# A decoder layer on one core: the feed-forward's up products by quarters, seven block products for eight, on 18 of 22 column pairs

## What is computed

```
h   = RMSNorm(x)
u   = causal_dwconv(h @ w_up, ffn_conv)        # w_up: 1024 x 5632, width 3
gate, up = split(u)                            # 2816 columns each
x   = x + RMSNorm((silu(gate) * up) @ w_down)  # w_down: 2816 x 1024
```

## Time and profile before

| | us |
|---|---|
| median of 3 runs | 1547.7 |
| lowest and highest | 1547.31, 1548.53 |
| the profiled execution, its own time | 1546.41 |
| its span, first to last instruction | 1544.7 |
| PE busy | 1502.6 |
| DVE busy | 898.1 |
| ACT busy | 655.0 |
| POOL busy | 179.3 |

### The profile page before, as it was taken

How to read it: one execution, slowest core, us unless ns; L and a number is a source line. 1 busy time by engine, 2 the same in 40 slices (tenths; PEclk the granted TensorE clock), 3 DMA queues, 4 the chain that set the end, 5 groups by cost and what they waited for, 6 DMA issues and landing times.

```text
span 1544.7 us, 19459 instructions
## 1 busy us (share of the span) xinstructions
PE 1502.6 (97%) x7515; PEld 1265.8 (82%) x7515; DVE 898.1 (58%) x1371; ACT 655.0 (42%) x1151; POOL 179.3 (12%) x200
## 2 busy tenths in 40 slices
PE   5999999999989999999999999999999999999996
PEld 4777888788879998878888888888888888888885
DVE  6675536360158885466876664335967666334666
ACT  5433456321247785355443333224333333224344
POOL 3000011000067772000100000000200000000110
PEclk8999999999989999999999999999999999999998
DMA  7542425636223332633323332333232333223222
GB/s 217 81 94 35 43 88 148 159 99 111 83 78 108 111 104 90 217 89 89 109 85 93 96 102 94 101 112 97 85 107 83 100 100 98 97 97 114 91 96 96
DMA packets 169657, 158.16 MB, mean 102 GB/s; under 512 B 19608, under 2 KB 131422, under 8 KB 169566
## 3 DMA queue, kind: packets, MB, share of 16 engines
q1 hardware_dynamic: 169312, 156.82, 36.2%
q10 hardware_dynamic: 254, 0.10, 0.0%
HBM read 134.88 MB, written 22.02 MB: 102 GB/s over the span
## 4 chain that ended last, share of the span: by engine, by line
PE 93%; DVE 2%; ACT 2%; DMA 1%; issue 1%; POOL 0%; SPq 0%; ACTq 0%; DVEq 0%; POOLq 0%
PE psum L1915 10%; PE psum L1914 10%; PE psum L1913 10%; PE psum L1839 9%; PE psum L1841 9%; PE psum L1840 9%; PE psum L559 5%; PE psum L561 5%; PE psum L560 5%; PE psum L1198 4%; PE psum L1252 3%; PE psum L614 3%; PE psum L616 3%; PE psum L615 3%; DMA w_raw<-in_w_in 1%
## 5 line engine op out<-in xcount | busy, mean ns | idle before, releaser
L144 DVE TENSOR_TENSOR w_wlo<-w_raw,w_whi 128x1024 fp32r<-128x1024 f32 x202 | 261.2, 1293 | 541.9 <-ACT w_whi L138 541.8
L138 ACT ACTIVATE w_whi<-w_raw 128x1024 fp32r<-128x1024 f32 x202 | 213.9, 1059 | 634.9 <-PE psum L1915 282.2
L1913 PE MATMUL psum<-m_hi,w_whi 128*128 128x512 f32 x704 | 274.2, 390 | 0.0
L1915 PE MATMUL psum<-m_hi,w_wlo 128*128 128x512 f32 x704 | 273.9, 389 | 0.0
L1914 PE MATMUL psum<-m_lo,w_whi 128*128 128x512 f32 x704 | 273.9, 389 | 0.0
L1839 PE MATMUL psum<-w_whi,m_hi 128*128 128x512 f32 x592 | 231.2, 391 | 1.6 <-DVE w_wlo L144 0.9
L1840 PE MATMUL psum<-w_wlo,m_hi 128*128 128x512 f32 x592 | 230.4, 389 | 0.0
L1841 PE MATMUL psum<-w_whi,m_lo 128*128 128x512 f32 x592 | 230.4, 389 | 0.0
L1915 PEld LDWEIGHTS psum<-m_hi,w_wlo 128*128 128x128 f32 x704 | 132.1, 188 | 27.4
L1913 PEld LDWEIGHTS psum<-m_hi,w_whi 128*128 128x128 f32 x704 | 132.1, 188 | 27.4
L1914 PEld LDWEIGHTS psum<-m_lo,w_whi 128*128 128x128 f32 x704 | 132.1, 188 | 27.3
(11 more groups left out here) (303 smaller groups left out, 2126.0 us busy)
## 6 DMA issues: line engine op xcount, KB each, us to landing
w_raw<-in_w_up SPq DMA_DIRECT2D x88, 512.0 KB, 3.9
w_raw<-in_w_down SPq DMA_DIRECT2D x44, 512.0 KB, 3.7
w_raw<-in_w_in SPq DMA_DIRECT2D x36, 512.0 KB, 6.2
w_raw<-in_w_out SPq DMA_DIRECT2D x16, 512.0 KB, 4.5
w_raw<-in_w_ple_gate SPq DMA_DIRECT2D x16, 512.0 KB, 3.9
gate_rows<-rows_stage SPq DMA_DIRECT2D x24, 256.0 KB, 2.1
x_tiles<-in_x SPq DMA_DIRECT2D x8, 512.0 KB, 8.5
x<-in_x SPq DMA_DIRECT2D x8, 512.0 KB, 6.1
```

What stands on the lines that cost most here:

```text
L138: act.activation(self.whi[j % self.RING][:], self.raw[j % self.RAW][:], ACT.Copy).then_inc(self.rounded, 1)
L144: dve.tensor_tensor(self.wlo[j % self.RING][:], self.raw[j % self.RAW][:], self.whi[j % self.RING][:].bitcast(F32), ALU.subtract).then_inc ...
L1913: pe.matmul(out, wh[:, part], hi[:, kt, :], start=(kt == 0), stop=False)
L1915: ins = pe.matmul(out, wl[:, part], hi[:, kt, :], start=False, stop=(kt == KT - 1))
```

## The change

The up products of 18 of the 22 column pairs are no longer made for one token half after the other, but for both together. The operands are cut in two along the inner dimension, the tokens, and gate against up, which gives blocks of 2 by 2 by 2, and the eight block products become seven with the sums of Winograd's form. PE works in pieces: a piece is one weight block of 128x512 by one block of h (or a sum of blocks), 4 inner blocks by 3 matmuls. A pair has seven pieces, in the order B11, T1, T2, B21, T3, B22, T4; the T are sums. New work for a pair: POOL makes four sums of weight blocks (`Units.sum`) and two joins of results (`pool_join`); DVE makes seven remainders of 128x512, five joins that read PSUM, four taps and one gate over 1024 tokens (`dve_pairs`); ACT makes seven roundings of 128x512, three copies out of PSUM, the first tap of both lines and silu (`act_pairs`). The ring holds four pieces: `round(n)` waits until piece n-4 is multiplied.

The other four pairs are done as before, half after half, ahead of the 18 (`pe_plain`, 16 tiles in 32 pieces of 12 matmuls), and there POOL makes the remainders of the weights. In this stretch DVE and ACT make the sums of h. f1 is transposed after tiles 6 and 8 of 16, kt 0 to 3 and kt 4 to 7; f0 in two parts before the last two slabs of the output projection.

The gated values go to DRAM (`g_rows`), and are loaded again by 256 KB, each block once for each token half, into four buffers (`w_sums`) from which they are split (`load_g`, `act_split`). The residual goes to DRAM and comes back too. The down products of the first half run over row slabs as before; those of the second half run over two column halves of `w_down`, each in 11 slabs of two row blocks, and the splits of all 22 blocks fall in the first column half, two a slab. x0 is transposed in the second column half.

The core of the diff:

```diff
+
+    def ring(self, j):
+
+        return (j + (j >= self.flip)) % self.RING
 
...
+    RING, RAWS, PLAIN = 4, 4, 4
+    TILES = 4 * PLAIN
+    PAIRS = FT - PLAIN
+    STEPS = 7
+    B11, T1, T2, B21, T3, B22, T4 = range(STEPS)
+    N_PLAIN = 2 * TILES
...
+    def sum(self, pool, s, which):
...
+        b11, b21, b12, b22 = (self.block(s, u, half) for u in range(2) for half in range(2))
+        sums, n = self.sums[s % 2], 4 * s
+        if which == self.T1:
+            for u in range(2):
+                self.landed(pool, self.tile(s, u))
...
+            ins = pool.tensor_tensor(sums[:, 0, :], b12, b11, ALU.subtract)
+        elif which == self.T2:
+            pool.wait_ge(self.made, n + 1)
+            ins = pool.tensor_tensor(sums[:, 1, :], sums[:, 0, :], b22, ALU.subtract)
+        elif which == self.T3:
+            ins = pool.tensor_tensor(b12, b22, b12, ALU.subtract)
+        else:
+            pool.wait_ge(self.made, n + 2)
+            pool.wait_ge(self.rest, self.STEPS * s + self.T1 + 1)
+            ins = pool.tensor_tensor(sums[:, 0, :], b21, sums[:, 1, :], ALU.add)
+        ins.then_inc(self.made, 1)
...
+    def round(self, act, n):
...
+        if n < self.RING:
+            self.multiplied.wait(act, ("slab", self.at - 2 + n // 2))
+        else:
+            self.multiplied.wait(act, ("unit", n - self.RING))
+        act.activation(self.home(n)[0], self.source(n), ACT.Copy).then_inc(self.rounded, 1)
...
+    def remainder(self, eng, n):
...
+        hi, lo = self.home(n)
+        eng.wait_ge(self.rounded, n + 1)
+        eng.tensor_tensor(lo, self.source(n), hi.bitcast(F32),
+                          ALU.subtract).then_inc(self.plain_rest if n < self.N_PLAIN else self.rest, 1)
...
                     self.pe_natural(pe, f"outp{half}", first["outp", half] + n * KT // 2 + i, (2 * i, 2 * i + 1), (n,),
                                     of(self.hi[half]), of(self.lo[half]), 0, KT - 1)
-        for half in range(2):
-            self.pe_up(pe, half)
-            for kt in range(FT):
-                slot = kt % KT
-                pe.wait_ge(s["split_lo"], half * FT + kt + 1)
-                ghi, glo = self.hi[half], self.lo[half]
-                self.pe_natural(pe, f"down{half}", first["down", half] + kt, (kt,), (0, 1),
-                                lambda _, t: ghi[:, slot, t * P:(t + 1) * P], lambda _, t: glo[:, slot, t * P:(t + 1) * P],
+        self.pe_plain(pe, 0)
+        self.pe_plain(pe, 1)
+        self.pe_pairs(pe)
+        for kt in range(FT):
+            pe.wait_ge(s["split_lo"], kt + 1)
+            self.pe_natural(pe, "down0", first["down", 0] + kt, (kt,), (0, 1), *self.g_halves(0), 0, FT - 1)
+        for n in range(2):
+            for i in range(FT // 2):
+                if n == 0:
+                    pe.wait_ge(s["split_lo"], FT + 2 * i + 2)
+                self.pe_natural(pe, "down1", first["down", 1] + n * FT // 2 + i, (2 * i, 2 * i + 1), (n,), *self.g_halves(1),
                                 0, FT - 1)
+                if n * FT // 2 + i in self.X0_TURNS:
+                    for group in self.added:
+                        pe.wait_ge(group, self.add_count("down0", self.HT - 1))
...
+    def pe_piece(self, pe, n, out, hi, lo, start, stop, *keys, fresh=None):
+
+        self.units.ready(pe, n)
+        wh, wl = self.units.home(n)
+        for kt in range(KT // 2):
+            if fresh:
+                fresh(kt)
+            part = slice(kt * P, (kt + 1) * P)
+            pe.matmul(out, wh[:, part], hi(kt), start=(start and kt == 0), stop=False)
+            pe.matmul(out, wh[:, part], lo(kt), start=False, stop=False)
+            ins = pe.matmul(out, wl[:, part], hi(kt), start=False, stop=(stop and kt == KT // 2 - 1))
+        self.multiplied.mark(ins, ("unit", n), *keys)
...
+    def pe_pairs(self, pe):
+        s, units = self.s, self.units
+        h = lambda half, at: (lambda kt: self.hi[half][:, at + kt, :], lambda kt: self.lo[half][:, at + kt, :])
+        two = lambda ap, at: (lambda kt: ap[:, at, kt, :], lambda kt: ap[:, at + 1, kt, :])
+        moving = {Units.B11: h(1, 0), Units.T1: two(self.s1, 0), Units.T2: two(self.s23, 0), Units.B21: h(1, 4),
+                  Units.T3: two(self.s23, 2), Units.B22: h(0, 0), Units.T4: h(0, 4)}
+        first_use = {Units.T1: 4, Units.T2: 8, Units.T3: 12, Units.B22: 16}
+        for c in range(Units.PAIRS):
+            for q in range(Units.STEPS):
+                key = ("pair", c, q)
+                out = self.banks.open(pe, key, (Units.STEPS * c + q) % 8)
+                if c == 0 and q in first_use:
+                    pe.wait_ge(s["sum_lo"], first_use[q])
+                self.pe_piece(pe, units.number(c, q), out, *moving[q], True, True, key)
...
+        self.act_plain(act)
+        self.act_pairs(act)
+        j = first["down", 0]
+        for kt in range(FT - 1):
+            slabs.round(act, j + kt + 2, m)
+            self.act_split(act, kt + 2)
+        for t in range(self.HT):
+            self.act_out(act, "down0", t, 0)
+        self.act_split(act, FT + 1)
+        j = first["down", 1]
+        slabs.round(act, j + 1, m)
+        for i in range(FT - 1):
+            slabs.round(act, j + i + 2, m)
+            if i + 1 < FT // 2:
+                self.act_split(act, FT + 2 * i + 2)
+                self.act_split(act, FT + 2 * i + 3)
...
+    def act_pairs(self, act):
+        s, units, m = self.s, self.units, self.multiplied
+        base, late = 2 * Units.PLAIN, slice(self.PAD + HALF, self.PAD + SEQ)
+        for c in range(Units.PAIRS):
+            n = units.number(c, 0)
+            if c == 0:
+                self.act_plain_line(act, 1, base - 1)
+            else:
+                self.act_tap_up(act, c - 1)
+                self.act_gate_line(act, c - 1)
+            units.round(act, n + 3)
+            key = ("pair", c, Units.B11)
+            m.wait(act, key)
+            if c:
+                self.banks.released(act, ("pair", c - 1, Units.T2))
+                act.wait_ge(s["joined"], 2 * c - 1)
+            self.banks.release(act.activation(self.copies[0][:], self.banks.of(key), ACT.Copy), key)
+            units.round(act, n + 4)
+            if c:
+                self.act_tap_gate(act, c - 1)
+            units.round(act, n + 5)
+            if c == 0:
+                self.act_smooth(act, base - 1, self.acc[0], self.FREED + 2 * base - 1)
+            else:
+                self.act_smooth(act, base + c - 1, self.long_acc[0], self.FREED + 2 * (base + c))
+            units.round(act, n + 6)
+            key = ("pair", c, Units.B21)
+            m.wait(act, key)
+            act.wait_ge(s["freed"], self.FREED + 2 * (base + c))
+            self.banks.release(act.activation(self.long_line[0][:, late], self.banks.of(key), ACT.Copy), key)
+            units.round(act, n + 7)
+            units.round(act, n + 8)
+            if c == Units.PAIRS - 1:
+                m.wait(act, ("unit", n + Units.T3))
+                self.slabs.round(act, self.first["down", 0], m)
+            units.round(act, n + 9)
+        c = Units.PAIRS - 1
+        self.act_tap_up(act, c)
+        self.act_gate_line(act, c)
+        self.slabs.round(act, self.first["down", 0] + 1, m)
+        self.act_tap_gate(act, c)
+        self.act_split(act, 0)
+        self.act_split(act, 1)
+        self.act_smooth(act, base + c, self.long_acc[0], self.FREED + 2 * (base + c + 1))
+
...
+    def act_gate_line(self, act, c):
+        key = ("pair", c, Units.T4)
+        self.multiplied.wait(act, key)
+        self.banks.release(act.activation(self.long_line[0][:, self.PAD:self.PAD + HALF], self.banks.of(key), ACT.Copy), key)
+
+    def act_tap_gate(self, act, c):
+        act.wait_ge(self.s["joined"], 2 * c + 2)
+        act.wait_ge(self.s["gated"], 2 * Units.PLAIN + c)
+        act.activation(self.long_acc[0][:], self.long_line[0][:, 0:SEQ], ACT.Copy,
+                       scale=self.first_tap(2 * Units.PLAIN + c, 0)).then_inc(self.s["tap0"], 1)
...
+        self.dve_plain(dve)
+        self.dve_pairs(dve)
+        j = first["down", 0]
+        for kt in range(FT - 1):
+            slabs.remainder(dve, j + kt + 2)
+            self.dve_split(dve, kt + 2)
+        for t in range(self.HT):
+            self.dve_out(dve, "down0", t, 1)
+        self.dve_split(dve, FT + 1)
+        j = first["down", 1]
+        slabs.remainder(dve, j + 1)
+        for i in range(FT - 1):
+            slabs.remainder(dve, j + i + 2)
+            if i + 1 < FT // 2:
+                self.dve_split(dve, FT + 2 * i + 2)
+                self.dve_split(dve, FT + 2 * i + 3)
...
+    def dve_pairs(self, dve):
+        s, units, m = self.s, self.units, self.multiplied
+        base = 2 * Units.PLAIN
+        late = slice(self.PAD + HALF, self.PAD + SEQ)
+        early = slice(self.PAD, self.PAD + HALF)
+        of, copy = self.banks.of, [tile[:] for tile in self.copies]
+        for c in range(Units.PAIRS):
+            n, last = units.number(c, 0), base + c - 1
```

(51 more changed lines are left out.)

671 lines of the change are left out of this document (492 added, 179 removed).

## The result

The changed kernel takes 1573.8 us (median of 4 runs, 1572.7 to 1575.9), the kernel before 1547.5: a ratio of 1.017, with a 95% interval of 1.0153 to 1.0188. It is slower by 26.3 us. The profiled executions differ by 27.0: 1573.44 us with a span of 1571.7 after, 1546.41 and 1544.7 before.

The account below looks back on a forecast made before the run. PE's matmul count was taken as the bound from 610 us on; -49.0 - 1.4 + 39 + 1.6 + 7.1 + 6 + 5 + 8.5 = +16.8 on 1546.4 gave 1563.2, or 1564 against the median, range 1548 to 1585.

Parts of the forecast that it names:

- rival 2: Every rest of PE brings the clock down, 19 us in place of 8.5: 1575 us; chance 0.16.
- matmuls removed: Up products of the 18 pairs: 216 fewer matmuls, nine slabs' worth at 5.44 us, -49.0 us.
- f0 in two parts: f0's transposes: a slab now stands between the two parts, removing PE's wait, -1.4 us (-2.1 to +1).
- ten waits for the splits: Second half's down products, slabs 1 to 10: PE waits 3.9 us each for DVE's splits, +39 us (36 to 42).
- entry into the second half: Slab 0 of the second down products: last split stands behind results taken from PSUM, +1.6 us (1.3 to 2.5).
- entry into the first down products: From the pairs into the down products: first split stands behind the last pair's join and taps, +7.1 us (6 to 9).
- inside the 18 pairs: DVE and POOL hinder each other in the pairs, 0.3 us a pair, +6 us (0 to 16).
- the plain pairs: Four plain pairs: f1's second half, the start and the entry to the pairs cost +5 us (0 to 12).
- slow clock: PE's eleven rests bring the granted clock down five times at 1.7 us each, +8.5 us (0 to 19).
- Rival 4: Second half's splits don't hold PE up, so 39 and most of the clock cost go: 1516 us; chance 0.07.
- Rival 3: POOL and DVE exclude each other through most of the pairs, 1.1 us more a pair: 1584 us; chance 0.11.
- DMA at nothing: Loads and stores of slabs, gated blocks and residual cost nothing; late residual loads would cost what they overrun.

Follow-up runs that it names:

- the loaded run: Three more unread POOL subtractions in 17 of the 18 pairs, against the changed kernel with reordered splits, entry and plain pairs: 1539.9 us, 32.1 more.
- e6_entry_alone: Against the changed kernel, ACT and DVE make the first two splits ahead of the last pair's taps, before the first down products: 1569.0 us.

## Why the prediction came out as it did

The forecast was slower, 1564, with a range of 1548 to 1585; 1573.8 lies in the range, 10 above the forecast, and next to rival 2's 1575. That it is no further off is in part luck: 6 us that the prediction had for the pairs did not come, and stand against 4.8 too few for the plain pairs and 14.1 too few for the clock. Rival 2's nearness has the same luck in it.

| term | predicted | traces |
|---|---|---|
| matmuls removed | -49.0 | -49.0; putting as many back cost 49.9 |
| f0 in two parts | -1.4 | -2.3 |
| ten waits for the splits | +39 | +39.6 |
| entry into the second half | +1.6 | +1.5 |
| entry into the first down products | +7.1 | +6.4 |
| inside the 18 pairs | +6 | 0 |
| the plain pairs | +5 | +9.8 |
| slow clock | +8.5 | +22.6 |
| start of the program | none | -1.7 |
| sum | +16.8 | +26.9 |

- **The waits: right, by their own chain.** From where a slab would have started to its start it is 3.83 us (4.06 from the last matmul, less 0.23), as worked out, of which the trace shows 3.67 as waiting; with the restart it is 3.96 (9.41 less 5.45, at full clock). ACT and DVE in the changed kernel, after slab 1 was done at 1278.6:

```profile
1278.68 1.06 ACT L142 ACTIVATE w_whi<-w_raw 128x1024 fp32r<-128x1024 f32 x1 [6.61 <-PE psum L2083]
1279.64 1.13 ACT L2468 ACTIVATE m_hi<-w_sums 128x512 fp32r<-128x512 f32 x2
```

```profile
1279.76 1.23 DVE L148 TENSOR_TENSOR w_wlo<-w_raw,w_whi 128x1024 fp32r<-128x1024 f32 x1 [8.58 <-ACT w_whi L142]
1280.91 1.29 DVE L2889 TENSOR_TENSOR m_lo<-w_sums,m_hi 128x512 fp32r<-128x512 f32 x2
```

The steps are the prediction's: rounding, remainder, two splits. It named ACT's order as the place, which was half of it: turning ACT's list round changed nothing, since DVE's has the same wait in front. The slabs stood 11.4 us apart and not the 9.3 that it named, by the clock. Rival 4, that the splits would be there in time, is dead.
- **The clock: the step that failed.** "I take five falls, +8.5": there were twelve, one behind each of the ten rests, one at the entry and one at f1, where the prediction had counted no rest; 22.6 us, 1.9 each on average, and above its upper bound of 19. The size of a fall, 1.7, was nearly right; the count was not, and the rows gave no ground for taking a half. The row that was there, a fall behind rests of 1.8 and 1.5 us among small matmuls, spoke for rival 2, which was given 0.16 and holds. The Trainium skill (TensorE: Matmul & The Clock Gate, HAM oscillation) describes bursts of matmuls between waits that each start at the low clock. The trace of after agrees in the main, 11.4 us a slab for 9.4: six of the ten slabs start at 0.50, and the other four fall to it within a microsecond. The runs with filled rests show that it is the rest that does it.
- **Inside the pairs: the account was right, the cost nothing.** The prediction had 18.1 of 19.0 us for DVE's and POOL's exclusive work with 3.5 of joins to fit beside it, and took 6 us in all. Between 791.08 and 1131.22 PE ran 1500 matmuls in 340.1 us, which is 0.227 each. Rival 3 is dead for this kernel; the loaded run shows that it begins 1.2 us a pair further on. The Trainium skill (SBUF — State Buffer, Who interferes with whom) says that the two exclude each other when DVE has two inputs in SBUF and POOL's instruction reads SBUF; the two splits of 3.48 us for 1.28 beside POOL's addition, and the joins from PSUM at their 0.68, agree.
- **The plain pairs: the term was mis-sized**, 9.8 for 5, within its 0 to 12. PE waits there seven times, 7.6 us in all. The chain of three instructions for each of f1's blocks cost 2.6 where 2.5 was taken; the waits for the weights' remainders, 3.6 on POOL and 1.3 on DVE, are together twice the 1 and 1.5 that stood for them in the prediction; 2.3 us lie beyond the waits, restarts among them, and were not broken down. Why is argued from the rows alone (DVE's and POOL's instructions made longer by each other, gates that stand late in DVE's list): earlier gates brought 0.4 us at most, and no run has POOL's load taken away there.
- **f0: mis-sized** by 0.9; both parts now run without a wait, and the whole of the -2.1 that the prediction gave as its end was gained.
- **DMA at nothing: right for this kernel,** but close. From 686 us on no wait of PE, ACT or DVE is for a DMA in the changed kernel; yet as soon as the first splits were moved ahead, in `e6_entry_alone`, ACT waited 2.94 us for the first gated block.

## What to carry to other kernels

Before a gain in matmuls is counted, look in each engine's list at what stands behind an instruction that waits for PE: one preparation step behind such a wait, in one list of two, cost here as much as the whole gain, and two slabs of lead instead of one gave it back. Price a repeated rest of PE with the slow clock behind it, here 1.9 us for each rest of 3.7; if the rest can't be avoided, a few matmuls that nobody needs are cheaper than the rest. And when work is moved to POOL, add up DVE's two-operand SBUF work and POOL's as if they were one engine's: here that sum came out above what was measured (22.0 us a pair for 20.9). When a step is moved ahead, look also at what it reads: the next thing to hold it here was a load.

## What the runs showed of the hardware that was not expected

- More matmuls made the kernel faster: 90 that nobody reads took it from 1573.8 to 1555.3 us.
- A rest of 2.77 us, repeated in the same place ten times, brought the clock down seven times. It is no fixed response to a rest of that length; what else decides was not looked into. The clock during the rest does not always show the fall: it is 1.00 in the whole of the rest before 1271.24, and 0.50 from 1272.
- Beside a loaded POOL, DVE was busy 94% of the pairs' time for 72% of work, and PE never waited. The busy share of DVE alone tells little of what it still can take: 3.9 us more of POOL's work a pair cost 32 us.
